# One gather of 8 KB rows in place of two of 4 KB: U and V of an expert fetched together into a ring of 8

## What is computed

```python
q = (xc @ w_pq).reshape(n, 8, 2, 128)             # 8 heads, two halves
s = einsum('nhpd,pkd->nhpk', q, sub_keys)         # 128 keys per half
s1, i1 = top_k(s[:, :, 0], 16);  s2, i2 = top_k(s[:, :, 1], 16)
cand = s1[..., :, None] + s2[..., None, :]        # 256 pairs per head
top_s, pos = top_k(cand, 16);  eid = expert number of pos   # i1*128 + i2
g = softmax(top_s)
act = gelu(einsum('nhkd,nd->nhk', u_tab[eid], xc))   # rows of 1024 floats
out = einsum('nhk,nhkd->nd', g * act, v_tab[eid])    # the same 128 experts
```

## Time and profile before

| | us |
|---|---|
| median of 3 runs | 3374.73 (3372.68 to 3376.29) |
| the profiled execution | 3375.08 |
| its span | 3373.3 |
| PE, DVE, POOL, ACT busy | 2574.5, 2570.2, 1985.7, 625.3 |
| packets of the software queue (the gathers) | 81.1% of 16 DMA engines' span |
| first gather issued at | 590.12 |
| gathers issued | 2064 |

### The profile page before, as it was taken

One profiled execution on the slowest core, in us unless ns is written; L12 is line 12 of the kernel. 1 busy time (PEld: TensorE's weight loads), 2 busy tenths in 40 slices (PEclk: granted clock), 3 DMA queues, 4 the chain that ended last, 5 costly groups with the idle time before them and its releaser, 6 DMA issues.

```text
span 3373.3 us, 27666 instructions
## 1 busy us (share of the span) xinstructions
PE 2574.5 (76%) x7810; PEld 1248.6 (37%) x7810; DVE 2570.2 (76%) x5694; ACT 625.3 (19%) x1400; POOL 1985.7 (59%) x2104
## 2 busy tenths in 40 slices
PE   6898898277778776877786778777877787787777
PEld 3555545134333333333333333333333333362222
DVE  4889894998887878787878787878788877757564
ACT  2332323111121112111111111111111111111111
POOL 1000000677777777777777777777777777757774
PEclk8999998589889889988899899898998998878999
DMA  6010005899999999999999999999999999989996
GB/s 202 19 37 19 28 31 190 315 394 409 409 409 406 409 407 408 400 409 402 405 404 409 400 409 399 409 407 404 404 408 402 409 399 409 402 305 404 409 409 265
DMA packets 318560, 1144.79 MB, mean 339 GB/s; under 512 B 37888, under 2 KB 41584, under 8 KB 317392
## 3 DMA queue, kind: packets, MB, share of 16 engines
q0 software_dynamic: 297216, 1082.26, 81.1%
q1 hardware_dynamic: 21208, 60.94, 5.1%
HBM read 1133.85 MB, written 10.72 MB: 339 GB/s over the span
## 4 chain that ended last, share of the span: by engine, by line
DMA 33%; POOL 18%; DVE 16%; PE 9%; issue 8%; ACT 0%; POOLq 0%; DVEq 0%
DMA arena<-in_peer_v_dram,arena 26%; POOL arena L1099 18%; DMA arena<-in_peer_u_dram,arena 7%; DVE arena L1371 5%; PE VA L1592 5%; DVE arena L1301 2%; DVE XP L1383 2%; DVE arena L1298 1%; PE QB L1628 1%; PE QB L1636 1%; PE QB L1572 1%; DVE arena L1305 1%; DVE arena L1339 1%; DVE arena L1336 1%; DVE arena L1340 1%
## 5 line engine op out<-in xcount | busy, mean ns | idle before, releaser
L1592 PE MATMUL VA<-arena 128*128 128x512 f32 x3032 | 1626.1, 677 | 686.5 <-DMA arena<-in_peer_v_dram,arena 604.3
L1371 DVE CUSTOM_DVE_ANT_0 arena<-arena,HP 128x1024 f32<-128x1024 f32 x1024 | 1233.3, 1218 | 572.2 <-DMA arena<-in_peer_u_dram,arena 567.7
L1099 POOL DMA_INDIRECT arena<-in_peer_u_dram,arena x1032 | 983.8, 953 | 430.3 <-issue 269.9
L1592 PEld LDWEIGHTS VA<-arena 128*128 128x128 f32 x3032 | 600.2, 213 | 1627.6 <-issue 1348.2
L1099 POOL DMA_INDIRECT arena<-in_peer_v_dram,arena x1032 | 980.4, 950 | 375.4 <-issue 264.3
L1172 ACT ACTIVATE arena<-ident,arena 128x128 f32<-128x128 f32 x758 | 281.8, 396 | 1250.8 <-PE VA L1592 1245.1
L1383 DVE SCALAR_TENSOR_TENSOR XP<-arena,XP 128x1024 f32<-128x1024 f32 x258 | 332.0, 1287 | 41.7 <-DMA arena<-in_peer_v_dram,arena 34.8
L623 DVE SCALAR_TENSOR_TENSOR arena<-arena 128x128 f32<-128x128 f32 x960 | 273.4, 347 | 7.9
L413 POOL COPY arena<-arena 128x1024 f32<-128x1024 f32 x8 | 8.3, 1040 | 453.9 <-DVE arena L643 453.9
L1572 PEld LDWEIGHTS QB<-arena 128*128 128x128 f32 x2048 | 239.2, 193 | 30.7 <-issue 30.7
L1572 PE MATMUL QB<-arena 128*128 128x128 f32 x2048 | 239.5, 276 | 2.6 <-PEq L190 2.6
(11 more groups left out here) (207 smaller groups left out, 1363.5 us busy)
## 6 DMA issues: line engine op xcount, KB each, us to landing
arena<-in_peer_u_dram,arena POOLq DMA_INDIRECT x1032, 11.6
arena<-in_peer_v_dram,arena POOLq DMA_INDIRECT x1032, 11.6
arena<-x SPq DMA_DIRECT2D x17, 512.0 KB, 7.0
arena<-in_x_prompt_dram SPq DMA_DIRECT2D x16, 512.0 KB
arena<-in_peer_wq_dram SPq DMA_DIRECT2D x8, 1024.0 KB, 14.6
arena<-in_w_in_dram SPq DMA_DIRECT2D x8, 896.0 KB, 13.2
x<-arena SPq DMA_DIRECT2D x8, 512.0 KB
arena<-in_w_ple_gate_dram SPq DMA_DIRECT2D x1, 4096.0 KB, 17.3
```

Source lines behind the costliest of these rows:

```text
L1099: nc.gpsimd.indirect_dma_start(rows[slot(turn)], None, table, bass.IndirectOffsetOnAxis(ap=index, axis=0)).then_inc(landed[slot(turn)], 16)
L1371: nc.vector.tensor_tensor_reduce(out=row, in0=row, in1=HP[:, :], scale=1.0, scalar=0.0, op0=ALU.mult, op1=ALU.add, accum_out=dots[:, t % 2 ...
L1592: last = nc.tensor.matmul(VA[:, c:c + BANK], diag[:, n % DIAGS, :], rows[slot(turn)][:, c:c + BANK], start=v_turn(t, k) == 0, stop=v_turn( ...
```

## The change

The two tables become one input, `peer_uv`, with the V row of an expert behind its U row (joined on the host before the launch). One gather per choice fetches 8 KB per token, so 1 MB, into a ring of 8 slots of 8 KB. `LAG` is gone: a choice's V half is added in its own turn. ACT therefore makes each weight by itself (`row_weight`: gelu of one column, times the gate, then the diagonal). DVE adds the V half of every fifth choice and of the last, two choices after its dot, PE the other 101 of a tile. The first tile is ranked in five parts, the first two of one head each. The finish of a tile moves from choices 37 to 60 up to choices 1 to 19 of the next tile; `h3` and `h3T` are gone, and `x2T` shares `hT`. The gate product's sigmoid is written back into `QB`. The samples' gathers come at choices 94 and 98, four each.

```diff
-RING = 13
-MAIN_ROWS = 12
-PARTS = 4
+RING = 8
+MAIN_ROWS = 7
-LAG = 40
-RANK_AT = (28, 68, 96, 124)
-RANK_FIRST_AT = (54, 78, 100, 124)
-U_SAMPLE, V_SAMPLE = 62, 78
+SAMPLE_AT = (94, 98)
+START = ((0, 1), (1, 1), (2, 2), (4, 2), (6, 2))
+STEADY = ((0, 2), (2, 2), (4, 2), (6, 2))
+RANK_AT = (30, 58, 86, 114)
+RANK_FIRST_AT = (46, 70, 92, 114)
...
+def by_vector(k):
+    return k % 5 == 0 or k == CHOICES - 1
...
+                freed[TURN[t, k]] = (vd_used, dve_count(t, k) + 1) if by_vector(k) else (vp_used, pe_count(t, k) + 1)
...
-            def gather(table, turn, index):
+            def gather(turn, index):
                 if turn >= RING:
                     pool.wait_ge(*freed[turn - RING])
-                nc.gpsimd.indirect_dma_start(rows[slot(turn)], None, table, bass.IndirectOffsetOnAxis(ap=index, axis=0)
+                nc.gpsimd.indirect_dma_start(rows[slot(turn)], None, peer_uv, bass.IndirectOffsetOnAxis(ap=index, axis=0)
                                              ).then_inc(landed[slot(turn)], 16)
...
-            def gelu_of(t, p):
-                part = slice(p * PICKS, (p + 1) * PICKS)
-                act.wait_ge(u_used, t * CHOICES + (p + 1) * PICKS)
-                nc.scalar.activation(gelu[:, part], dots[:, t % 2, part], ACT.Gelu).then_inc(gelu_ready, 1)
-
-            def diagonal(t, k):
+            def row_weight(t, k):
+                dot = dots[:, k:k + 1]
+                act.wait_ge(dots_ready, t * CHOICES + k + 1)
+                steps.link(nc.scalar.activation(dot, dot, ACT.Gelu))
+                if k == 0 or part_of_row(t, k) != part_of_row(t, k - 1):
+                    act.wait_ge(gates_ready, part_no(t, part_of_row(t, k)) + 1)
+                nc.scalar.activation(dot, dot, ACT.Copy, scale=gates[:, t % 2, k:k + 1]).then_inc(weights_ready, 1)
+                if by_vector(k):
+                    return
                 n = pe_count(t, k)
                 if n >= DIAGS:
                     act.wait_ge(vp_used, n - DIAGS + 1)
-                act.wait_ge(weights_ready, t * PARTS + k // PICKS + 1)
-                nc.scalar.activation(diag[:, n % DIAGS, :], ident[:, :], ACT.Copy,
-                                     scale=weights[:, t % 2, k:k + 1]).then_inc(diag_ready, 1)
+                act.wait_ge(weights_ready, t * CHOICES + k + 1)
+                nc.scalar.activation(diag[:, n % DIAGS, :], ident[:, :], ACT.Copy, scale=dot).then_inc(diag_ready, 1)
...
                     dot(t, j)
-                    if v_of(t, j) and by_vector(*v_of(t, j)):
-                        add_row(*v_of(t, j))
+                    if j >= 2 and by_vector(j - 2):
+                        add_row(t, j - 2)
...
-                        if j == 44:
-                            turn_x2(f, P)
+                        if j == 4:
+                            turn_x2(f, P)
                         for quarter in range(4):
-                            if j == 49 + 2 * quarter:
+                            if j == 8 + 2 * quarter:
                                 gate_product(f, P, quarter // 2 * BANK, quarter % 2 * (KD // 2))
...
+                        for chunk in range(CHUNKS):
+                            if j == 30 + 4 * chunk:
+                                sample_queries(chunk)
```

More of the change, by code:

```diff
@@ L80, in count_turns @@
         for j in range(CHOICES):
[L81 to L104, removed]
+            if t == LAST and j in SAMPLE_AT:
+                first = SAMPLE_AT.index(j) * NB // GROUPS
+                for b in range(first, first + NB // GROUPS):
+                    sample[b], n = n, n + 1
+            turns[t, j], n = n, n + 1
+    return turns, sample
+TURN, S_TURN = count_turns()
 class Chain:
@@ L1269, in _ @@
[L1269 to L1277 removed]
+                        if j in SAMPLE_AT:
+                            first = SAMPLE_AT.index(j) * NB // GROUPS
+                            some = slice(first, first + NB // GROUPS)
+                            act.wait_ge(dots8_ready, some.stop)
+                            nc.scalar.activation(gelu8[:, some], dots8[:, some], ACT.Gelu).then_inc(gelu8_ready, 1)
@@ L1359, in weigh @@
-            def weigh(t, p):
-                part = slice(p * PICKS, (p + 1) * PICKS)
-                dve.wait_ge(gates_ready, gate_count(t, p))
-                dve.wait_ge(gelu_ready, t * PARTS + p + 1 + (t == LAST and p > 1))
-                TT(weights[:, t % 2, part], gates[:, t % 2, part], gelu[:, part], ALU.mult).then_inc(weights_ready, 1)
+                head, heads = parts_of(q)[p]
+                these = slice(head, head + heads)
+                pairs = cand[:, 0:heads, :].rearrange("p h (i j) -> p h i j", j=TOPK)
@@ L1365, in dot @@
             def dot(t, k):
-                turn = U_TURN[t, k]
-                row = rows[slot(turn)]
+                turn = TURN[t, k]
                 if k == 0:
@@ L1498, in _ @@
-                    if q == SAMPLE:
-                        if j == 33:
+                    for qp in parts_at(t, j, "lists"):
+                        choose_lists(*qp)
+                    for qp in parts_at(t, j, "pairs"):
+                        choose_pairs(*qp)
+                    for qp in parts_at(t, j, "names"):
+                        name_experts(*qp)
+                        if qp != (0, 1):
+                            normalise_gates(*qp)
+                    if t == 0 and j == 3:
+                        normalise_gates(0, 1)
@@ L1560, in turn_h, with queries @@
                 last.then_inc(hnT_ready, 1)
[L1562 to L1563 removed]
+            def queries(q, p, half):
+                n, (head, heads) = part_no(q, p), parts_of(q)[p]
+                bank = n % 2 * BANK
                 pe.wait_ge(hT_copied, q + 1)
@@ L1566, in queries @@
                     pe.wait_ge(sc_copied, n - 1)
-                if after_finish:
-                    pe.wait_ge(fin_copied, after_finish)
-                for a in range(first, first + LISTS // 2):
-                    m = p * LISTS + a
+                for a in range(half * heads, (half + 1) * heads):
+                    m = 2 * head + a
                     for k in range(KD):
@@ L1715, in _ @@
+                    if j and not by_vector(j - 1):
+                        add_row(t, j - 1)
             turn_x2(LAST, P)
```

597 lines of the change are left out of this document (272 added, 325 removed).

## The result

The changed kernel takes 3316.03 us (median of 4 runs, 3312.68 to 3319.23) against 3374.04 for the kernel before on the same chip: a ratio of 0.983, with a 95% interval of 0.981 to 0.984. It is faster, as forecast, and the time lies within the range; it is 25 us above the predicted 3291. The profiled execution took 3319.23 us, with a span of 3317.5, so 55.8 us of span were won where the sum had 84. By the medians it is 58.0 us: the profiled execution is the slowest of the four.

A forecast was written before the change was run, and what follows sets the result against it. The DMA engines' rate was taken to set the pace between about 700 and 3340 us. The terms -63 - 11 - 11 + 7 - 8 + 2 = -84 took 3375.1 to 3291 us, range 3248 to 3361.

The forecast's parts named there:

- Term 1: All gathers: 8 KB rows in place of 4 KB raise the rate from 409 to 419 GB/s, -63 us.
- Rival A: Gathers: each 8 KB row may be cut into two 4 KB packets, rate stays 409 GB/s, 3354 us; chance 0.14.
- Terms 2 and 3: Start: a one-head first part brings the first gather forward, -11 us; tile 0 loses less at 600 to 700 us, -11 us.
- Term 4: Steady tiles: eight slots cover 10 us of lateness, the finish is the tight place; 1 us lost per finished tile, +7 us.
- Rival B: Finish: the ring is too short if PE gets the lower clock, 23 us lost per tile, 3445 us; chance 0.10.
- Term 5: Last tile's samples: query chunks spread among V rows, late indices covered by POOL's lead and transfers in flight, -8 us.
- Term 6: The end: a dot and two ACT steps precede the last V row after the last landing, +2 us.

The follow-up runs named there:

- split44: The changed kernel with each choice fetched by two gathers of 4 KB rows (U, then V) into the same ring slot: 3374.91 us.
- start4: The changed kernel with the first tile ranked in four parts of two heads, as the other tiles are: 3326.42 us.
- best2: The changed kernel with every fourth V half on DVE, PE's blocks cut up, samples' chain earlier and in pairs, gate product spread over choices 8 to 18: 3276.57 us.
- ring7: The changed kernel with a ring of 7 slots in place of 8: 3409.98 us.
- s_chain: The changed kernel with only the samples' ranking chain 2 to 6 choices earlier, their gathers still in two fours: 3316.36 us.

## Why the prediction was right, and where it was not

- **Term 1, the row size, held.** Taken: 409 to 419 GB/s, -63 us. Shown: 410 to 420, 63 us by the rates and 59 between split44 and the changed kernel. Rival A falls with it: packets of 8 KB are moved whole by the software queue. The Trainium skill ("DMA: Bandwidth & Descriptors", section "SWDGE vs HWDGE vs iDMA") prefers packets of at most 4096 bytes; here rows in packets of 8 KB moved at 420 GB/s and in packets of 4 KB at 410. Rival A's time was wrong as well: at 410 GB/s it is not 3354 but 3374.9 us (split44), so of the 21 us that the other terms were to win nothing is left.
- **Terms 2 and 3, the start, held.** First gather at 577.1 (579 forecast). 600 to 700 us at 415 GB/s, better than the 390 that was to show it: the 117 us of DVE work did fit into 49 choices. Start and tile 0 together gave 31.1 us for 29.8, and start4 puts 10 us on the small first part.
- **Term 4, the ring, was mis-sized.** +7 us was taken, 1 per tile, with 56 as the far end. A tile took 331.8 us against 329.4 forecast, so 16 us more over six tiles; against best2's 328.0 the changed ring loses 3.8 us per tile, some 23 in six. The step that failed is "the tight place is the finish": it reckoned PE's lag there alone, from zero, and called it "just under the cover". But the queries of each ranking part, which it did not reckon against the cover at all, put PE behind as well, and V rows that are already late use up the cover before the next block comes. ring7 shows how thin it was: 2.5 us less of it cost 94 us. Rival B's mechanism, a ring too short, was there in small. In the finish PE had the full clock, as reckoned, and not 0.63; but ahead of the queries it came back from its pauses at 0.50, 2.5 us of lag in the part shown. B's 23 us of loss per tile did not come. The prediction's ground against a low clock, that 0.61 was seen only while PE was mostly idle, misread its own rows: the earlier trace rows has 0.61 with PE busy 9.66 of 12 us.
- **Term 5, the samples, was wrong in sign.** -8 us was taken, with +8 as the bad end; the last 136 choices came out 16 us worse than the sum in the profiled execution (10 in start4's), where about 3 would be term 4's. The sample queries themselves lost less than the 12 reckoned: 2990 to 3090 us moved 395 GB/s, 100 x (1 - 395/420) = 6 us. The step that failed is "what it waits beyond that the transfers in flight cover". The 9.8 us wait for indices was there, but s_chain, where it is gone, is no faster; the wait that the change adds on ACT, four sample dots ahead of every later weight, was never listed, nor that the four sample rows take half of the ring's slots while it lasts.
- **Term 6** was +2 and came out at -0.5.
- **The range.** Its lower end takes 11 us for tile 0 and the samples, where the middles of their good ends give 4 and 4.5; 3248 would be 3250, which changes nothing.

So the mechanism held and carried the whole gain, and the total was missed by 28 us of span in two terms that both speak of the same thing: what a slot waits for besides its transfer.

## What to carry to other kernels

When gathers set the pace, ask for the row size first: 10 GB/s more was the whole gain of this large change, and all else in it summed to zero. Then price the ring by running the consumer's lag on from block to block (queries, V rows, finish) and not stage by stage from zero, and with the clock that the engine has after a pause; if the cover is near the largest lag, move a little work to the other engine and cut the blocks before anything else. And list, for each wait on a group, what stands behind it in the same engine's queue: a group of four in a ring of eight stops the other four.

## What the runs showed of the hardware

In the same kernel and order, indirect rows of 4 KB moved at 410 GB/s at a DMA share of 1.03 and rows of 8 KB at 420 at 1.01. A packet of 8 KB took 319.7 ns of an engine in the mean, two of 4 KB 329.7. After a pause of 5.21 us PE came back at a granted clock of 0.50, and a V row took 3.78 us in place of 1.98. Taking V rows from PE does not shorten it in proportion: from 101 to 85 rows per tile a V-row matmul went from 671 to 705 ns, while the granted clock over the span fell from 0.894 to 0.869 of 2.4 GHz.
